# First-norm modulation of a two-layer trunk: sixteen dot-product tiles turned into 512-wide products in 32 columns of TensorE

## The reference, cut to what matters

```
mod = silu(cond) @ w_ada + b_ada          # (1024) @ (1024 x 9*1024), per layer and condition
sh1, sc1, g1, ... = mod
h = rmsnorm(x, norm_ffn1) * (1 + sc1) + sh1
x = x + 0.5 * g1 * swiglu(h, ...)
```

## Time and profile before

| | us |
|---|---|
| median of 3 runs (2062.28 to 2065.17) | 2063.63 |
| the profiled execution's own time | 2058.96 |
| its span, first to last instruction | 2057.1 |
| TensorE busy | 1945.5 (95%) |
| DVE busy | 1440.2 (70%) |
| first large product starts at | 48.02 |

### The profile page before, as it was taken

How to read it: one execution, slowest core, us unless ns; L and a number is a source line. 1 busy time by engine, 2 the same in 40 slices (tenths; PEclk the granted TensorE clock), 3 DMA queues, 4 the chain that set the end, 5 groups by cost and what they waited for, 6 DMA issues and landing times.

```text
span 2057.1 us, 28940 instructions
## 1 busy us (share of the span) xinstructions
PE 1945.5 (95%) x11000; PEld 1864.7 (91%) x11000; DVE 1440.2 (70%) x2290; ACT 787.5 (38%) x1301; POOL 332.9 (16%) x295
## 2 busy tenths in 40 slices
PE   6999998999879999999999999989997899999998
PEld 6999997778768999999999999978886799999998
DVE  7888889566664567888888888865656555674444
ACT  3323235334333254332353333542444324533333
POOL 2301014210002221010131110321000121210002
PEclk9999999999989999999999999989999899999999
DMA  7767664232212236666575666432322223543332
GB/s 304 256 229 229 226 218 138 87 105 90 77 52 90 98 129 205 215 202 206 169 244 193 200 197 209 153 100 80 108 78 73 69 91 103 192 158 130 125 123 82
DMA packets 82830, 310.07 MB, mean 151 GB/s; under 512 B 9460, under 2 KB 10922, under 8 KB 81952
## 3 DMA queue, kind: packets, MB, share of 16 engines
q1 hardware_dynamic: 80064, 298.77, 43.4%
q0 software_dynamic: 2656, 9.85, 1.5%
HBM read 305.70 MB, written 2.88 MB: 150 GB/s over the span
## 4 chain that ended last, share of the span: by engine, by line
PE 83%; DVE 10%; ACT 4%; issue 2%; DMA 1%; SPq 0%; POOL 0%; DVEq 0%; ACTq 0%; POOLq 0%
PE bank L1463 46%; PE ps_att L1463 26%; PE ps_br L1463 2%; DVE lo L864 1%; PE ps_att L1712 1%; PE ps_att L1703 1%; ACT hi L612 1%; PE ps_o L1730 1%; DVE tiny L1248 1%; ACT pr L795 1%; DVE pr L1272 1%; DVE areaO L984 1%; DVE areaG L1299 1%; DVE pr L1269 1%; DVE areaE L1283 1%
## 5 line engine op out<-in xcount | busy, mean ns | idle before, releaser
L612 ACT ACTIVATE hi<-raw 128x1024 fp32r<-128x1024 f32 (+1 forms) x396 | 432.5, 1093 | 595.8 <-PE bank L1463 328.6
L864 DVE TENSOR_TENSOR lo<-raw,hi 128x1024 fp32r<-128x1024 f32 (+1 forms) x396 | 529.1, 1337 | 116.1 <-ACT hi L612 115.3
L1463 PE MATMUL bank<-h_hi,hi 128*128 128x384 f32 (+1 forms) x1536 | 544.2, 354 | 18.9 <-POOL h_lo L1372 8.7
L1463 PE MATMUL bank<-h_lo,hi 128*128 128x384 f32 (+1 forms) x1536 | 525.1, 342 | 0.0
L1463 PE MATMUL bank<-h_hi,lo 128*128 128x384 f32 (+1 forms) x1536 | 524.8, 342 | 0.0
L1463 PEld LDWEIGHTS bank<-h_hi,hi 128*128 128x128 f32 x1536 | 296.0, 193 | 49.6 <-issue 34.0
L1463 PEld LDWEIGHTS bank<-h_lo,hi 128*128 128x128 f32 x1536 | 296.1, 193 | 1.3
L1463 PEld LDWEIGHTS bank<-h_hi,lo 128*128 128x128 f32 x1536 | 295.3, 192 | 0.0
L1463 PE MATMUL ps_att<-h_hi,hi 128*128 128x386 f32 (+1 forms) x736 | 248.8, 338 | 1.1 <-DVE lo L864 1.1
L1463 PE MATMUL ps_att<-h_hi,lo 128*128 128x386 f32 (+1 forms) x736 | 248.5, 338 | 0.0
L1349 POOL TENSOR_TENSOR g_lo<-areaF,g_hi 128x384 f32 x88 | 107.6, 1223 | 870.7 <-ACT g_hi L691 870.7
(11 more groups left out here) (255 smaller groups left out, 2613.7 us busy)
## 6 DMA issues: line engine op xcount, KB each, us to landing
raw<-w_main SPq DMA_DIRECT2D x332, 512.0 KB, 4.0
areaM<-w_ada SPq DMA_DIRECT2D x134, 512.0 KB, 3.3
raw<-w_fused SPq DMA_DIRECT2D x64, 640.0 KB, 3.9
areaG<-w_ada SPq DMA_DIRECT2D x7, 512.0 KB, 12.3
areaO<-c_rep SPq DMA_DIRECT2D x3, 1024.0 KB, 6.1
areaE<-bias POOLq DMA_DIRECT2D x2, 1024.0 KB, 6.2
x<-x_in SPq DMA_DIRECT2D x1, 1536.0 KB, 9.1
areaE<-w_ada SPq DMA_DIRECT2D x3, 512.0 KB, 15.4
```

Source lines behind the costliest of these rows:

```text
L612: act.activation(hi[:, slot, 0:width(base)], raw[:, slot, 0:width(base)], ACT.Copy).then_inc(hi_ready, 1)
L864: dve.tensor_tensor(lo[:, slot, 0:w], raw[:, slot, 0:w], hi[:, slot, 0:w].bitcast(F32), ALU.subtract).then_inc(lo_ready, 1)
L1463: last = pe.matmul(dst, wt[:, slot, w], ac[:, c, 0:cols], start=c == 0 and k == 0, stop=c == chunks - 1 and k == 2)
```

## The change

All 16 tiles go to TensorE with the operands exchanged. The conditions become stationary: `c_pad` holds, for each of the 8 channel blocks, 32 columns of which two are the conditions and 30 are zero (a memset on DVE, and the Silu of ACT into the two columns). The weights move, 512 wide. The host lays the tiles out so that tile m = 4q + i holds channel blocks 2i and 2i+1 for the 512 outputs of group q. Tile i of a group writes to partitions 32i to 32i+31 of one PSUM bank, `ps_att[:, q, :]`, so a bank ends with four partial sums. ACT copies the bank to `head_rows` (`head_evict`), and `head_columns` adds the four partial sums and turns rows into columns in one step: each 128x128 piece of `head_rows` is stationary, and `pick`, 128x2 with ones at the rows of either condition, moves. All 16 columns then lie in `ps_br` and one DVE copy brings them to `mod`.

The DVE dot products of the head are gone. The conditions on all partitions are still needed by later modulation tiles: `c_rep` is loaded behind raw tile 3, and its Silu runs on ACT behind `affine`. Eight buffers hold the tiles, loaded in one order with raw tiles 0 and 1 between. DVE's `split` of tile 2 moves behind `scaled(1)`, and ACT's three splits stand between its copies of the banks.

```diff
-HEAD_PE = 7
+HEAD_SLOTS = 8
@@ buffers
-        head_pe = [areaG[:, 1024 * i:1024 * (i + 1)] for i in range(6)]
-        head_dve = [area[:, 1024 * i:1024 * (i + 1)] for area in (areaM, areaE) for i in range(3)]
+        head_raw = [areaG[:, 1024 * i:1024 * (i + 1)] for i in range(6)] + [areaM[:, 1024 * i:1024 * (i + 1)] for i in range(2)]
+        head_rows = areaE[:, 0:2048].rearrange("p (q k) -> p q k", q=4)
+        c_pad = kt[:, 0, 0:32 * C].rearrange("p (c m) -> p c m", m=32)
+        pick = kt[:, 1, 0:2]
@@ SP
-            sp.dma_start(areaO[:, 0:2048], c_rep).then_inc(rows_in, 16)
-            for j in range(ADA_FIRST - HEAD_PE):
-                if j < HEAD_PE:
-                    if j >= 6:
-                        sp.wait_ge(head_pe_done, j - 5)
-                    sp.dma_start(head_pe[j % 6], w_ada[j]).then_inc(head_pe_in[j % 6], 16)
-                if j >= 6:
-                    sp.wait_ge(head_dots, j - 5)
-                    load(j - 6, w_main[j - 6])
-                sp.dma_start(head_dve[j % 6], w_ada[HEAD_PE + j]).then_inc(head_dve_in[j % 6], 16)
+            for m in range(ADA_FIRST):
+                if m >= HEAD_SLOTS:
+                    sp.wait_ge(head_used, m - HEAD_SLOTS + 1)
+                sp.dma_start(head_raw[m % HEAD_SLOTS], w_ada[m]).then_inc(head_in[m % HEAD_SLOTS], 16)
+                if m in (7, 11):
+                    load(m // 4 - 1, w_main[m // 4 - 1])
+            load(2, w_main[2])
@@ SP, in the loop of later loads
+                if n == 3:
+                    sp.dma_start(areaO[:, 0:2048], c_rep).then_inc(rows_in, 16)
@@ ACT
-            act.activation(c_act[...], vv[:, V_COND:V_COND + 2 * C], ACT.Silu).then_inc(cond_act, 1)
-            act.wait_ge(rows_in, 16)
-            act.activation(areaO[:, 0:2048], areaO[:, 0:2048], ACT.Silu).then_inc(rows_act, 1)
+            act.wait_ge(pad_zero, 1)
+            act.activation(c_pad[:, :, 0:2], vv[...], ACT.Silu).then_inc(cond_act, 1)
+            def head_evict(q):
+                act.wait_ge(head_used, 4 * q + 4)
+                act.activation(head_rows[:, q, :], ps_att[:, q, :], ACT.Copy).then_inc(head_row, 1)
@@ ACT, norm
                     act.activation(tiny[:, 4:8], tiny[:, 0:4], ACT.Exp).then_inc(lam_exp, 1)
+                    head_evict(0)
                     act.preload_act_table(ACT.Sqrt)
...
                 act.preload_act_table(ACT.Silu)
-                for n in range(AHEAD):
-                    split(n)
+                head_evict(1)
+                split(0)
+                head_evict(2)
+                split(1)
+                head_evict(3)
+                split(2)
                 for c in range(C):
                     affine(p, c)
...
+                act.wait_ge(rows_in, 16)
+                act.activation(areaO[:, 0:2048], areaO[:, 0:2048], ACT.Silu).then_inc(rows_act, 1)
@@ DVE
+            dve.memset(kt[:, 0, 0:32 * C], 0.0).then_inc(pad_zero, 1)
@@ DVE, norm (the loop over nine tiles of two dot products each goes)
+                    dve.wait_ge(consts_in, 32)
+                    dve.tensor_reduce(pick, ident.rearrange("p (i m) -> p m i", m=32)[:, 0:2, :], AX_X, ALU.add).then_inc(pick_ready, 1)
+                    lambdas()
+                    reciprocal_root()
+                    for n in range(AHEAD - 1):
+                        split(n)
+                    dve.wait_ge(head_done, 1)
+                    dve.tensor_copy(mod[:, 0:ADA_FIRST, :], ps_br[:, 0:2 * ADA_FIRST].rearrange("p (a g) -> p a g", g=2)).then_inc(head_mod, 1)
                     scale_and_shift(p)
...
                 scaled(0)
                 scaled(1)
+                split(AHEAD - 1)
@@ POOL, layer_loads
-                    pool.wait_ge(head_dots, ADA_FIRST - HEAD_PE)
+                    pool.wait_ge(head_mod, 1)
@@ PE
+            def head_modulation(q):
+                for i in range(4):
+                    m = 4 * q + i
+                    pe.wait_ge(head_in[m % HEAD_SLOTS], 16 * (m // HEAD_SLOTS + 1))
+                    for k in range(2):
+                        last = pe.matmul(ps_att[32 * i:32 * i + 32, q, :], c_pad[:, 2 * i + k, :],
+                                         head_raw[m % HEAD_SLOTS][:, 512 * k:512 * k + 512], start=k == 0, stop=k == 1)
+                    last.then_inc(head_used, 1)
+            def head_columns(q):
+                pe.wait_ge(head_row, q + 1)
+                for i in range(4):
+                    a = 8 * q + 2 * i
+                    last = pe.matmul(ps_br[:, a:a + 2], head_rows[:, q, P * i:P * (i + 1)], pick, start=True, stop=True)
+                if q == 3:
+                    last.then_inc(head_done, 1)
@@ PE, norm
-                    for j in range(HEAD_PE):
-                        head_modulation(j)
-                        if j == 3:
-                            square_sums(k)
+                    head_modulation(0)
+                    head_modulation(1)
+                    square_sums(k)
+                    pe.wait_ge(pick_ready, 1)
+                    head_columns(0)
+                    head_modulation(2)
                     rstd(k)
+                    head_columns(1)
+                    head_modulation(3)
+                    head_columns(2)
+                    head_columns(3)
```

More of the change, by code:

```diff
@@ L344, in build @@
         modb = sb("modb", [P, 2, C, 2])
-        c_act = sb("c_act", [P, C, 2])
         kt = sb("kt", [P, 5, 512])
@@ L435, in build @@
         cond_act, rows_in, rows_act = sem("cond_act"), sem("rows_in"), sem("rows_act")
-        head_pe_in, head_dve_in = [sem(f"head_pe_in{i}") for i in range(6)], [sem(f"head_dve_in{i}") for i in range(6)]
-        head_pe_done, head_dots, head_mod = sem("head_pe_done"), sem("head_dots"), sem("head_mod")
+        head_in = [sem(f"head_in{i}") for i in range(HEAD_SLOTS)]
+        pad_zero, head_used, head_row = sem("pad_zero"), sem("head_used"), sem("head_row")
+        pick_ready, head_done, head_mod = sem("pick_ready"), sem("head_done"), sem("head_mod")
         sq_sum = sem("sq_sum")
@@ L615, in _ @@
             act.wait_ge(vecs_in, 32)
-            act.activation(c_act[:, :, :].rearrange("p c g -> p (c g)"), vv[:, V_COND:V_COND + 2 * C], ACT.Silu).then_inc(cond_act, 1)
-            act.wait_ge(rows_in, 16)
-            act.activation(areaO[:, 0:2048], areaO[:, 0:2048], ACT.Silu).then_inc(rows_act, 1)
+            act.wait_ge(pad_zero, 1)
+            act.activation(c_pad[:, :, 0:2], vv[:, V_COND:V_COND + 2 * C].rearrange("p (c g) -> p c g", g=2), ACT.Silu).then_inc(cond_act, 1)
+            def head_evict(q):
+                act.wait_ge(head_used, 4 * q + 4)
+                act.activation(head_rows[:, q, :], ps_att[:, q, :], ACT.Copy).then_inc(head_row, 1)
             def x_square(c, drained_at):
@@ L888, in modulation @@
                     dve.wait_ge(head_mod, 1)
-                    dve.wait_ge(head_dots, ADA_FIRST - HEAD_PE)
                 else:
@@ L977, in norm @@
                 if k == 0:
-                    dve.wait_ge(rows_act, 1)
-                    for j in range(ADA_FIRST - HEAD_PE):
-                        dve.wait_ge(head_dve_in[j % 6], 16 * (j // 6 + 1))
-                        if j:
-                            dve.wait_ge(head_dots, j)
-                        for g, out in enumerate((products, head_dve[j % 6])):
-                            last = dve.scalar_tensor_tensor(out, head_dve[j % 6], 1.0, cond_rows[:, g, :], ALU.mult, ALU.mult,
-                                                            accum_out=mod[:, HEAD_PE + j, g:g + 1])
-                        last.then_inc(head_dots, 1)
-                        if j == 3:
-                            lambdas()
-                        if j == 5:
-                            reciprocal_root()
-                        if j >= 6:
-                            split(j - 6)
-                    dve.wait_ge(head_pe_done, HEAD_PE)
-                    dve.tensor_copy(mod[:, 0:HEAD_PE, :], ps_t[:, 0:2 * HEAD_PE].rearrange("p (a g) -> p a g", g=2)).then_inc(head_mod, 1)
+                    dve.wait_ge(consts_in, 32)
[6 more added lines that the diff above has]
+                    dve.tensor_copy(mod[:, 0:ADA_FIRST, :], ps_br[:, 0:2 * ADA_FIRST].rearrange("p (a g) -> p a g", g=2)).then_inc(head_mod, 1)
                     scale_and_shift(p)
@@ L1471, in part_of @@
                 return range(C // PARTS * step[-1], C // PARTS * (step[-1] + 1))
-            def head_modulation(j):
-                pe.wait_ge(head_pe_in[j % 6], 16 * (j // 6 + 1))
-                for c in range(C):
-                    last = pe.matmul(ps_t[:, 2 * j:2 * j + 2], head_pe[j % 6][:, P * c:P * (c + 1)], c_act[:, c, :], start=c == 0, stop=c == C - 1)
-                last.then_inc(head_pe_done, 1)
+            def head_modulation(q):
[13 more added lines that the diff above has]
+                    last.then_inc(head_done, 1)
             def square_sums(k):
@@ L1909 @@
```

(3 more changed lines are left out.)

1 line of the change is left out of this document (removed).

## The result

| | before | after |
|---|---|---|
| median, run side by side (5 runs each) | 2063.63 (2059.88 to 2069.70) | 2053.02 (2051.40 to 2053.85) |
| the profiled execution's own time | 2058.96 | 2053.30 |
| its span | 2057.1 | 2051.5 |
| copy to `mod` starts at | 44.10 | 35.85 |
| first large product starts at | 48.02 | 40.25 |

The ratio is 0.994, 95% interval 0.992 to 0.996: faster, by 10.6 us from median to median and 12.4 by the ratio. What follows goes by stages and by many runs, not by those two executions.

The account below looks back on a forecast made before the run. TensorE was taken as the bound, busy 95% of the span, with DVE's dot products holding the head; copy 6.4 us earlier less 0.6 given back is 5.8, so 2063.63 - 5.8 = 2057.8 us, range 2055.0 to 2064.0.

Parts of the forecast that it names:

- The bound of the head: Head: DVE's dot products hold the chain from 14.33 to the copy at 44.10 us; the DMA queue is second limit.
- The strips: Head tiles on TensorE: four 32-column strips run side by side, so a tile has 5.1 us and TensorE follows the DMA.
- the first rival: Head: strips do not overlap, 1.73 us a tile at best, copy at 51.3, 2071.5 us in all; chance 0.08.
- The program-order rival: Head: passes start only in program order; 1.30 us a tile, or 2.6 and 2083 us at low level (chance 0.03).
- wide products at the high level and narrow ones at the low: Head on TensorE: mixed clock case, narrow passes at 0.216 us, copy to `mod` at 37.7, 6.4 us earlier.
- The prediction's own bound for that case: Head: if narrow products also run at the high level, copy at 36.0 and net gain 7.5 us.
- Given back: Between copy and first large product: the moved split of tile 2 makes the first cast 0.63 us later; net 5.8 us.
- Moves what follows with it, nearly whole: After the head: bringing the first large product forward moves everything behind it nearly as much; net gain 5.8 us.
- What costs nothing here: List of edits said to add no time: memset, small reduction, later Silu of `c_rep`, ACT's splits, POOL's wait, queue after the head.
- Timed by TensorE and not by the clock on the wall: After the head: TensorE sets the time of what follows; its two waits for DVE's `lo` sum to 3.0 us.
- The low level throughout: Rival for the head: TensorE's clock stays low, only 2.2 to 4.1 us gained, 2060.5 us; chance 0.13.
- The gain lost later: Rival for the first feed-forward: a transfer or DVE times it, not TensorE, so 2063.6 us; chance 0.09.

Follow-up runs that it names:

- e3: The changed kernel with all four tiles of a group in the same 32-column strip; 1.0001 (0.9982 to 1.002) of the kernel before.
- e8: The changed kernel with raw tiles 0 and 1 four tiles later in the queue, ACT's copy and DVE's splits reordered; 0.995 of the kernel before, median 2051.97 us.
- e2: The changed kernel, unedited, profiled and run a second time; 0.9945 (0.9923 to 0.9967) of the kernel before, median 2053.99 us.
- e6: The changed kernel with `c_act` kept but unused, so later tiles keep their old addresses; 0.9969 (0.9955 to 0.9983) of the kernel before.
- e7: The kernel before with `c_act` moved behind all other tiles, so they lie 64 bytes lower; 0.9983 (0.9968 to 0.9999) of the kernel before.
- e4: The changed kernel with five unread wide products in the pause behind the last head columns; 0.9929 of the kernel before, median 2050.66 us.
- e13: The kernel before with a 1.4 us TensorE pause in layer 0's second feed-forward, ahead of layer 1's attention; 0.9987 (0.9970 to 1.0004) of the kernel before.

## Why the prediction was right or wrong

**The bound of the head, right.** DVE's chain of dot products was what ended last; without it TensorE and the DMA set the head. First wide product, seventh tile, last tile: 10.38, 21.15 and 32.03 against 10.5, 21.2 and 32.3. The order of the pieces is that of the chain.

**The strips, right.** Overlap was taken from two halves and holds for four strips; e3 shows what it is worth, 10.4 us at the copy. In the price of the first rival one figure is off: its narrow terms, 2.7 + 1.6 + 6.9, lose 5.6 us at the high level and not "some 4". e3's copy at 46.27 lies 5.0 below the rival's 51.3. The program-order rival falls by the passes that start at 17.96 and 17.98, where the code issues the last pass of tile 5 (in `areaG`, 17.98) ahead of the first of tile 6 (in `areaM`, 17.96), and by e8's four tiles in 2.81 us, 0.70 each, where that rival allows no less than 1.30. The Trainium skill's rule of strict order (TensorE: Matmul & The Clock Gate, "Part 3: Packing small matmuls") disagrees with the trace here as it did in the earlier trace rows.

**The narrow passes, mis-sized.** The step "wide products at the high level and narrow ones at the low" took 0.216 us a pass from the earlier trace rows. They took 0.12. In before they ran alone and never got faster; here they stand between wide ones and ran at the high level. The prediction's own bound for that case put the copy at 36.0; it came at 35.85, 1.85 us before the 37.7 of the forecast, and at 35.70 to 36.95 in the other traces of this head (in e2, the latest, the clock column reads 0.66 from 24 to 29 us).

**Given back, right.** The moved `split` costs 0.5 (0.6 forecast). The 18 products behind it take as long with either head, 4.95 to 5.96 and 4.99 to 5.87 us; TensorE had stood still for 6.9 us before them in before (41.16 to 48.02) and stands still for 4.4 now. Net lead at the first tile of 48: 7.0 us in after, 7.3 in e6, 8.0 in the mean of the traces, against 5.8 forecast and the prediction's 7.5 for narrow products at the high level.

**"Moves what follows with it, nearly whole", incomplete.** With the addresses kept (e6) it is right to 0.1 us over 2000 us in one pair of executions, and within the intervals over the runs: 6.4 us gained (3.5 to 9.3). The step that failed is the list in "What costs nothing here": it leaves out that `c_act` goes and that all tiles behind it move 64 bytes. (The diff shown with the change leaves out that line too: `-        c_act = sb("c_act", [P, C, 2])`.) That costs 0.65 us in each feed-forward behind layer 0's attention (1.2 ns for each of the 528 products there that move `g`, six rows of 88), and yet gains 3.5 us by e7; that the delay is what gains is what the 17 traces show, by the distance from the clock's last rise, and what the runs support only in part. "Timed by TensorE and not by the clock on the wall" is what hides it: TensorE's pace is itself not constant, it has stretches at the low level in the attention stages, and their sum depends on when its pauses come. With the head alone, the lead of 7.3 to 8.0 us gives 2063.63 - 7.3 = 2056.3 or 2055.6, both in the range; e6's median is 2056.76. The rest, to 2053.02, is put down to the addresses: 3.5 us by e7 (0.2 to 6.6). That the five runs also fell low by chance is not ruled out, though e2's ratio, 0.9945, is nearly the same.

**The other rivals.** The low level throughout was wrong, by the clock column. The gain lost later was half right in a way not meant: some 4 us of it are lost in layer 0's attention and 5 found again in layer 1's, in after's profiled run.

**Left open.** Why 64 bytes slow these products, and only past the first feed-forward (the mean distance of their starts in after is 173.3 ns up to 300 us, as in before, and 174.7 from 840 to 960 us), was not found; that the pace follows the addresses and not the head is shown by e6 and e7. Nor is it settled which pause of the attention stage is the one that decides, or how often an execution meets the short way: after is in the second row of the table of distances and e2, the same kernel, in the last.

## What to carry to other kernels

Narrow products are priced by what stands beside them on TensorE: alone they ran at 0.216 us, between wide ones at 0.12. A removed buffer is a change of every address behind it, so keep the old layout (one line, e6) when a change of a few microseconds is to be judged. And where executions of one kernel lie 8 us apart, read stages from marks in the trace, and gains from many runs. A difference of 0.7 us between two traces was no cost of the change here: five traces of one head differ among themselves by 1.0 us at that place.

## What the runs showed of the hardware

- Four strips of 32 columns run side by side with different moving data, fp32, 512 wide: four tiles in 4.07 us while they landed (after), in 2.81 when they had landed earlier (e8), in 6.98 in one strip (e3).
- A product of the same shape (moving `g`, 128x384) took 336 ns (median) instead of 334 after a shift of 64 bytes, in two kernels with different heads.
- A pause of 4.4 us behind the head let the clock fall (0.52 from 39 to 46 us), and the next 18 products took 5.87 us; wide products into one strip kept it at 1.00 (e4).
- The same attention stage took 440.3, 435, 440.6 or 443 us as it began 695.0, 696.1 to 696.8, 698.2 or some 596 us behind the clock's last rise, with either addresses in the last case and in the second (17 traces).
- A kernel with 1.4 us of work added had five of twelve runs over 3 us below the lowest of 29 runs without it (e13).
